# An encoder trunk on one core: value products with high and low halves side by side, and attention loops written out

## What is computed

```python
# layer 0, per 128 queries: keys up to the own chunk, selection by an indexer (a mask here)
logits = einsum('bthd,btkd->bhtk', qb, ks) * HEAD_DIM ** -0.5 + bias
p = softmax(where(valid, logits, -inf));  out = einsum('bhtk,btkd->bthd', p, vs)
# layer 1, per chunk of 64 queries: keys of the own and the previous chunk only
logits = einsum('bnqkgd,bnskd->bnkgqs', qb, kb) * HEAD_DIM ** -0.5 + bias
p = softmax(concat([where(kvalid, logits, -inf), sink]))[..., :-1]
out = einsum('bnkgqs,bnskd->bnqkgd', p, vb)
# each: mixer output @ w_out, then h + rms_norm(...), then square(relu(xn @ w1)) @ w2
```

## Time and profile before

| | us |
|---|---|
| median of 3 runs (2811.2 to 2813.43) | 2811.43 |
| the profiled execution | 2811.78 |
| its span in the trace | 2809.7 |
| PE busy, share of the span | 2636.1, 94% |
| DVE busy | 1509.3, 54% |
| ACT busy | 1005.1, 36% |
| POOL busy | 751.9, 27% |
| granted TensorE clock, mean of the span | 0.975 |

### The profile page before, as it was taken

The page is one execution under the profiler, slowest core; times in us unless marked ns, Lnnn a source line. Parts: engine busy times, 40 slices in busy tenths (PEclk is TensorE's granted clock), DMA queues, the critical chain, the costliest instruction groups (busy, mean ns, idle before and its releaser), DMA issues. The chain is left out here.

```text
span 2809.7 us, 36526 instructions
## 1 busy us (share of the span) xinstructions
PE 2636.1 (94%) x12584; PEld 2146.7 (76%) x12584; DVE 1509.3 (54%) x2879; ACT 1005.1 (36%) x1819; POOL 751.9 (27%) x369
## 2 busy tenths in 40 slices
PE   7899997998998999999999999868999999999998
PEld 6599775776776878888888887656677888888886
DVE  5599999765665653344333454255565334433335
ACT  5534433655553432211222143265643221122212
POOL 2013785234232122222222212311222222222220
PEclk9999997999999999999999999999999999999999
DMA  4462535433536421111111135543442111111113
GB/s 145 68 113 48 142 96 177 119 98 81 148 102 214 150 91 52 46 52 40 57 45 52 45 113 158 131 112 103 120 165 98 45 53 45 52 45 45 52 38 120
DMA packets 260043, 258.17 MB, mean 92 GB/s; under 512 B 11906, under 2 KB 219810, under 8 KB 257620
## 3 DMA queue, kind: packets, MB, share of 16 engines
q1 hardware_dynamic: 250436, 239.22, 29.6%
q10 hardware_dynamic: 9216, 16.78, 2.1%
q0 software_dynamic: 272, 0.62, 0.1%
HBM read 181.60 MB, written 74.97 MB: 91 GB/s over the span
## 5 line engine op out<-in xcount | busy, mean ns | idle before, releaser
L405 PE MATMUL ps<-xn_T,w_split 128*128 128x512 f32 x4608 | 1053.4, 390 | 1.6 <-DVE xn_T L1515 1.5
L405 PEld LDWEIGHTS ps<-xn_T,w_split 128*128 128x128 f32 x4608 | 863.6, 188 | 185.0 <-issue 2.9
L362 POOL TENSOR_TENSOR w_split<-w_raw,w_split 128x1024 fp32r<-128x1024 f32 x192 | 465.2, 2433 | 1494.9 <-ACT w_split L355 1494.6
L405 PE MATMUL ps<-w_split,hidden 128*128 128x512 f32 x3648 | 833.7, 390 | 7.5 <-POOL w_split L362 6.2
L405 PEld LDWEIGHTS ps<-w_split,hidden 128*128 128x128 f32 x3648 | 685.1, 188 | 151.1 <-issue 6.6
L1792 DVE TENSOR_TENSOR acc<-acc,ps 128x512 f32<-128x512 f32 x504 | 344.5, 687 | 332.6 <-PE ps L405 332.5
L355 ACT ACTIVATE w_split<-w_raw 128x1024 fp32r<-128x1024 f32 x192 | 197.8, 1050 | 599.8 <-PE ps L405 591.7
L1802 DVE TENSOR_TENSOR sq_h<-relu_h 128x512 f32<-128x512 f32 x128 | 88.6, 692 | 504.4 <-ACT relu_h L1340 504.4
L1340 ACT ACTIVATE relu_h<-ps 128x512 f32<-128x512 f32 x128 | 76.7, 599 | 448.9 <-PE ps L405 446.0
L1739 DVE TENSOR_TENSOR probs_T<-ps,probs_T 128x512 fp32r<-128x512 f32 x204 | 140.5, 690 | 154.8 <-ACT probs_T L1297 154.5
L405 PE MATMUL ps<-probs_T,v_split 128*64 128x512 f32 x612 | 192.7, 424 | 23.9 <-DVE probs_T L1739 23.6
(11 more groups left out here) (164 smaller groups left out, 2131.6 us busy)
## 6 DMA issues: line engine op xcount, KB each, us to landing
w_raw<-in_w SPq DMA_DIRECT2D x128, 512.0 KB, 4.0
q_scratch<-q_split SPq DMA_DIRECT2D x128, 128.0 KB, 2.4
q_tile<-q_scratch ACTq DMA_DIRECT2D x64, 256.0 KB, 2.7
cat_scratch<-attn_out_split SPq DMA_DIRECT2D x128, 128.0 KB, 2.4
w_raw<-in_w_in SPq DMA_DIRECT2D x30, 512.0 KB, 4.6
unit_tile<-cat_scratch SPq DMA_DIRECT2D x48, 256.0 KB, 3.5
h_scratch<-acc SPq DMA_DIRECT2D x24, 512.0 KB, 4.1
h_in<-h_scratch SPq DMA_DIRECT2D x24, 512.0 KB, 5.9
```

The lines of the kernel that those rows point to most:

```text
L362: nc.gpsimd.tensor_tensor(whl[:, n0 % 4, 1, :], wraw[:, n0 % 4, :], whl[:, n0 % 4, 0, :].bitcast(F32), ALU.subtract).then_inc(w_lo, 1)
L405: return nc.tensor.matmul(out_ap, stat, mov, start=start, stop=stop)
```

## The change

The loops of both layers are written apart (`pe_attn0`, `pe_attn1` and so on). What differs:

- **Value products.** The high and low halves of the values lie side by side, so one stationary operand of 128 columns gives rows 0-63 (high values) and 64-127 (low values) of bank 6 at once. A key block takes two matmuls, by the high and the low probabilities, in place of three. The inverse sums are transposed to 128 rows, and DVE's multiplication has 128 rows. POOL then has a copy of rows 64-127 to rows 0-63, a subtraction and an addition in place of one subtraction.
- **Layer 0.** The denominators use banks 4 and 5 in turn with the probabilities. Two logits heads go ahead of the transposes, the other two stand behind the second and third; DVE does two heads first and puts its low-part subtraction between the far and the near part of the others. ACT rounds the output of the last step inside the next one, behind the first to third block. Fills 0 to 15 are taken out by ACT. SP's `after_fill` stands ahead of its spill. POOL's mask and bias run three steps ahead.
- **Layer 1.** Logits are 192 wide (128 in tile 0), in three banks, with three heads ahead; denominators have bank 3. Probabilities are transposed as 64 keys (a new copy of the values, `v_odd_chunk`, shifted by a chunk) and 128 keys. The 64-key block has its high part in rows 0-63 and its low part in rows 64-127 of one operand, for one matmul; a step has 3 value matmuls (2 in tile 0) in place of 6 (3). The rounding of the output moves from ACT to POOL, which has four operations a step.

```diff
@@ constants and tiles @@
-LEAD = [1, 1]
+WIDTH1 = [P if b == 0 else P + CHUNK for b in range(NB)]
+LEAD0 = 2
+LEAD1 = 3
-    v2 = at("v_split", [P, 2, NB, HD], F32R, XT0 + 56 * K)
+    v2 = at("v_split", [P, NB, 2, HD], F32R, XT0 + 56 * K)
+    vodd = at("v_odd_chunk", [P, 2, NB, 2, HD], F32R, XT0 + 33 * K)
@@ sp_attn @@
-                spill(i, b)
                 for k in FILL[layer][i, b]:
                     after_fill(k)
+                spill(i, b)
@@ POOL, layer 0 and layer 1 @@
+            pool.wait_ge(o_ok, g + 1)
+            nc.gpsimd.tensor_copy(olo[:, s, :], osb[HD:P, s, :]).then_inc(o_low, 1)
...
+            nc.gpsimd.tensor_tensor(osb[0:HD, s, :], osb[0:HD, s, :], ohl[:, s, 0, :].bitcast(F32), ALU.subtract).then_inc(o_rest, 1)
...
+            nc.gpsimd.tensor_tensor(ohl[:, s, 1, :], osb[0:HD, s, :], olo[:, s, :], ALU.add).then_inc(ol_ok, 1)
...
+            nc.gpsimd.tensor_copy(olo1[:, s, :], osb1[HD:P, s, :]).then_inc(s1_low, 1)
...
+            nc.gpsimd.tensor_copy(ohl1[:, s, 0, :], osb1[0:HD, s, :]).then_inc(s1_hi, 1)
...
@@ act_attn0 @@
+            for st in range(KEYS0[b]):
...
+                nc.scalar.activation(pT[:, x % 4, 0, :], ps[:, 4 + y % 2, :], ACT.Copy).then_inc(c_hi, 1)
+                if todo and st >= 1:
+                    exps(g + 1, todo.pop(0))
+                if st == 2 and len(fills) == 2:
+                    take_fill(fills[0])
+                if g and st == min(2, KEYS0[b] - 1):
+                    out_high(g - 1)
+            act.wait_ge(d_full, g + 1)
...
+            for j in todo:
+                exps(g + 1, j)
+            if fills:
+                take_fill(fills[-1])
@@ act_attn1 @@
+            if g % NB:
...
+                nc.scalar.activation(pS1[0:HD, s, :], ps[0:HD, 4 + q % 2, :], ACT.Copy).then_inc(t1_hi, 1)
...
+            nc.scalar.activation(pL1[:, s, 0, :], ps[:, 4 + q % 2, :], ACT.Copy).then_inc(t1_hi, 1)
+            if g + 1 < HG * NB:
+                for j in range(4):
+                    exps(g + 1, j)
+            act.wait_ge(d1_full, g + 1)
...
@@ dve_attn0 @@
+            for _ in range(LEAD0 if todo else 0):
...
+            for st in range(KEYS0[b]):
+                j = todo.pop(0) if st and todo else None
+                if j is not None:
+                    far(g + 1, j)
+                probs_low(g, st)
+                if j is not None:
+                    near(g + 1, j)
@@ dve_attn1 @@
+            dve.wait_ge(e1_ok, 4 * g + 4)
+            nc.vector.reciprocal(rinv[:, s, :], rsum[:, s, :]).then_inc(r1_ok, 1)
+            for _ in range(LEAD1 if todo else 0):
+                logits(g + 1, todo.pop(0))
+            if g % NB:
+                probs_low(pS1[HD:P, s, :], ps[0:HD, 4 + q % 2, :], pS1[0:HD, s, :], q)
...
+            probs_low(pL1[:, s, 1, :], ps[:, 4 + q % 2, :], pL1[:, s, 0, :], q)
...
+            if g >= 2:
+                dve.wait_ge(s1_ok, g - 1)
+            nc.vector.tensor_tensor(osb1[:, s, :], ps[:, 6, :], rec1[:, s, :], ALU.mult).then_inc(o1_ok, 1)
@@ PE, values of layer 0 @@
-            mm(o, vv[:, 0, kt, :], probs[:, q % 4, 0, :], st == 0, False)
-            mm(o, vv[:, 0, kt, :], probs[:, q % 4, 1, :], False, False)
-            mm(o, vv[:, 1, kt, :], probs[:, q % 4, 0, :], False, st == keys[b] - 1).then_inc(pv_done, 1)
+            mm(ps[:, 6, :], vv, pT[:, x % 4, 0, :], st == 0, False)
+            mm(ps[:, 6, :], vv, pT[:, x % 4, 1, :], False, st == KEYS0[g % NB] - 1).then_inc(pv_done, 1)
@@ pe_attn1 @@
+            for _ in range(LEAD1 if todo else 0):
+                logits(g + 1, todo.pop(0))
+            for k in fills:
+                fill(pe, fu1, T_O1, k, 0, 2)
+            pe.wait_ge(e1_ok, 4 * g + 4)
...
+            for j in todo:
+                logits(g + 1, j)
+            denominators(g)
...
+                mm(o, value_pair(vodd[:, kv], b - 1), pS1[:, s, :], True, False)
+            for k in fills:
+                fill(pe, fu1, T_O1, k, 2, 4)
...
+            mm(o, value_pair(v2b[:, kv], b), pL1[:, s, 0, :], b == 0, False)
+            mm(o, value_pair(v2b[:, kv], b), pL1[:, s, 1, :], False, True).then_inc(o1_full, 1)
```

728 lines of the change are left out of this document (384 added, 344 removed).

## The result

The changed kernel takes 2762.16 us (median of 4 runs, 2760.9 to 2765.54), the kernel before beside it 2811.9 (2811.2 to 2813.43): a ratio of 0.9824, 95% interval 0.9807 to 0.9841. The gain is 49.7 us, where 61 were forecast: the sign and the range held, the size was 11 us too large. The profiled execution took 2762.01 us, with a span of 2760.2 against 2809.7 before.

The account below looks back on a forecast made before the run. Layer 1's 16 unfilled steps were taken as bound by a chain through the denominators, its 14 filled ones by PE, layer 0 between. 2811.78 - 31 (layer 0) - 29.6 (layer 1) = 2751 us, range 2724 to 2778.

Parts of the forecast that it names:

- nearly all from PE's shorter work; gaps gone and gaps new cancel: Layer 0, 31 steps: 385.9 us to 354.6, 31.3 gained, credited to fewer value matmuls (32.8 us).
- The wider load: Value matmuls: the stationary operand growing from 64 to 128 columns was costed at nothing.
- Step (2, 1): Layer 0, group 2, tile 1: sized like every tile 1, at 6.7 us.
- Tiles 5 and 6: Layer 0: tile 5 at 16.2 or 16.7 us; tile 6 at 17.5 with fills, 13.8 without.
- Tiles 2 and 3: Layer 0: tile 2 at 9.4 and 8.7 us, tile 3 at 11.3 in groups 0 and 1, 10.55 in 2 and 3.
- Tiles 0 and 1, and 7 without fills,: Layer 0: tile 0 at 3.5 us, tile 1 at 6.7, tile 7 without fills at 13.6 against 16.5 to 17.2.
- Unfilled steps of layer 1: First 16 steps: period from 6.39 to 4.6 us, POOL becoming the bound; 28.7 us gained.
- The first fill of layer 1: Layer 1, units return behind the spill of step (1, 7): gap grows to about 8 us, loss 1.9 us.
- Filled steps: Layer 1, last 14 steps: period 6.35 us against 6.70, with PE waiting for DVE's low part; 4.9 us gained.
- layer 0 keeps its time: Rival: leading heads and ACT's fills open gaps in every tile; layer 0 gains 10, total 2772 us; chance 0.17.
- The dear copy: Rival, layer 1: POOL's copies cost as much as its subtraction; layer 1 gains 7, total 2774 us; chance 0.12.
- the fourth rival: Clock falls: layer 1 stays at 1.2 GHz after PE's idle stretches, total 2860 us; chance 0.03.

Follow-up runs that it names:

- Experiment 1: Kernel before, without the product of the values' low with the probabilities' high part, two value matmuls per key block in both layers: 2802.82 us, ratio 0.9961.
- experiment 2: Changed kernel with the second value matmul of each layer 0 block issued twice (144 matmuls more): 2783.09 us, ratio 0.9898.
- Experiment 3: Changed kernel, POOL's weight splits ahead of the output's low part: in all four steps 2764.54 us; ahead of its output operations in (1, 7) 2759.61, (1, 6) and (1, 7) 2756.04.
- Experiment 4: Changed kernel with one leading logits head in layer 0 instead of two: 2759.87 us; one only in tiles 3, 5 and 6: 2753.71 us.
- experiment 5: Changed kernel with fills 0 to 15 of layer 0 taken out of PSUM by DVE instead of ACT: 2760.78 us, ratio 0.981.
- experiment 7: Changed kernel with POOL's output copy in layer 1 moving 64 of 512 columns from the third step on: 2761.49 us, ratio 0.9812.
- experiment 6: Changed kernel with ACT taking layer 1's denominators behind the first exponential again, not the fourth: 2759.95 us, ratio 0.9811.

## Why the prediction was right in sign and too large

- **Layer 0, the step that failed: "nearly all from PE's shorter work; gaps gone and gaps new cancel".** Experiment 1 gives that work 12 us in the old order, experiment 2 gives it 18.8 in the new one; not 32.8 in either. The gaps did not cancel, they grew: PE waits 30.4 us for DVE's low parts in the changed kernel, where it was 16.1. Over the 31 steps PE's busy time fell by 28.4 us (354.4 to 326.0), and its idle time rose by 13.0 (31.5 to 44.5). The 15.9 us that are missing are 8.4 in step (2, 1), 10.5 over the other steps, less 3.0 that I had left for the reload of stored fills and that was not lost. My sum also has a slip: for group 1 the pieces as printed give 86.4 us, not 87.8, so they would have forecast 1.4 us more still.
- **The wider load, put at nothing.** That isn't quite so. The load of a stationary operand of the values takes 191 ns on average with 128 columns, 139 with 64, and behind a wait two value matmuls take 0.73 us in place of 0.68. The changed kernel has 54 such pairs in layer 0: an estimate of 54 x 0.05 = 2.7 us, if all of it lies in the path. Where matmuls follow one another without a wait no difference shows (0.62 us at least with either).
- **Step (2, 1).** I had moved ACT's part of the weight split, "starts that about 1.4 us earlier now", and not followed POOL's: its queue had got three output operations for one ahead of the splits, with a wait for ACT's rounding of a step later. The earlier trace rows showed PE in such a wait for POOL's splits, at another place. Experiment 3 shows the cause, by the variant that turns both pairs: 6.4 us of that step.
- **Tiles 5 and 6** were under-sized by 0.3 to 1.4 us each, most of all tile 6 (18.2 to 18.9 with fills against 17.5, 15.1 against 13.8). Experiment 4 puts 0.8 to 1.0 of each on the second leading head, which I had charged to tile 3 alone. Tile 7 with fills came at 16.6 to 16.8 against 15.5; no run says why. Tiles 2 and 3, with fills taken by ACT, came at 9.65 and 11.68 against 9.4 and 11.3; the mechanism I gave is confirmed by experiment 5 (1.24 and 0.82 us). PE's wait for `part_sum` in layer 0 didn't go, as I had said it would: it is 3.6 us for ACT and 1.7 for DVE, against 5.5 for DVE before.
- **Tiles 0 and 1, and 7 without fills,** came near: 3.31 to 3.83 (3.5), 6.78 to 7.28 (6.7, in all but (2, 1)), 12.7 and 13.7 (13.6).
- **Unfilled steps of layer 1**: 4.43 us on average for the regular ones, against 4.6. The number was near, two of its reasons were not, so there was luck in it. POOL does not bind (experiment 7): its sum of 4.6 held four waits of 0.2 where its operations follow one another in 0.07 to 0.08 us, so that its own work comes to about 4.0. DVE's loop, which I had at 4.2, is the one that shows. And the denominators did not leave the chain by ACT's order (experiment 6). The term for the copy was right: 0.609 us measured, 0.6 taken.
- The Trainium skill (GPSIMD Engine Reference, 3.1 Elementwise — side-by-side cycle accounting) gives 769 ns as the best case of a loop over 512 elements; by that the copy would have been dearer. The measured copy of 64x512 takes 609 ns and decides.
- **The first fill of layer 1**: 7.25 us of wait against "about 8", a loss of 0.6 against 1.9. The spill follows its result 2.0 us later than before (4.77 against 2.78), where I had 2.2, and PE starts 3.7 us behind the first load's issue where it took 4.4. **Filled steps**: 6.38 against 6.35, PE waiting 0.42 for DVE's low part of 64 rows as walked; only the reason that they gain at all was wrong: they were no more bound by PE than the unfilled ones.
- **Ends**: the stretches between and behind the attentions lost 2.7 us, 3.4 were forecast (1.3 and 1.0 between, 1.1 behind).
- **The rivals.** Of the first, "layer 0 keeps its time", the threshold was 370 us, and it came to 370.5 with 15.4 us gained, nearer to the rival's 10 than to the forecast's 31; without the one step it would have been 364. The dear copy did not come. The clock did not cost what the fourth rival feared: it was 0.97 in the unfilled stretch of layer 1 (0.91 before), 1.00 in the filled one, and 0.77 around the first fill, as before. In layer 0 it was at 0.50 in two short stretches, one of them that of (2, 1). That layer 1 gained 36.2 where 31.7 were forecast is what kept the total within 11 us: two errors that cancel in part, not one right sum.

What stays open: how the 9.5 us that layer 0 has beyond experiment 1 (373.9 to the 364.4 with both splits ahead) divide between the order, the rounding that ACT does no longer in the path and the denominators in the probability banks. No run takes one of these alone. Nor does any run divide the 36 us of layer 1: experiment 1 shows that fewer value matmuls alone leave its periods as they were, but PE's new order, the three leading heads, the narrower logits (192 columns for 256) and the rounding moved to POOL came together.

## What to carry to other kernels

A stage in which an engine is busy 97% of the time may still be a chain that its work is spread over: before work taken off is counted as time, ask which wait ends last. Where engines hand blocks to and fro only part of it is time: between a third and somewhat over a half here (12.0 and 18.8 of 32.8 us). When an engine gets more operations per step, walk its queue past everything that stands behind them in the rare steps too (here a weight split in four of 32 steps), since one such place cost a fifth as much as the whole forecast gain of the stage. An order that is good for one block length needn't be for the next: a lead chosen per tile took layer 0 to 365.2 us, from 369.1 with one head and 370.5 with two everywhere.
